# The even layer of a two-block transformer kernel: three stages merged into one that works between the halves of its projection

## What is computed

```
h = x @ w_in                                   # 1024 x 2816
qa, ka, va, ga, qb, kb, vb = split(h)          # qa, ka, va, ga, qb: 512 columns each; kb, vb: 128 each
qa, ka = rope(qa), rope(ka) * 128 ** -0.5      # 4 retention heads of 128
ya = bidirectional_retention(qa, ka, va, decay_logit)
ya = group_norm(ya) * gn_gain * silu(ga)
qb, kb = rope(qb) * 64 ** -0.5, rope(kb)       # 8 query heads of 64, 2 key heads
yb = window_attention_with_sink(qb, kb, vb, sink_logit)
return concatenate([ya, yb]) @ w_out
```

## Time and profile before

| | us |
|---|---|
| median of 3 runs | 2055.55 |
| lowest, highest | 2055.08, 2060.99 |
| the profiled execution | 2063.12 |
| its span, first to last instruction | 2061.2 |
| PE, DVE, ACT, POOL busy in the span | 1800.1, 686.5, 421.5, 81.6 |
| PE's mean granted clock, of full speed | 0.935 |

### The profile page before, as it was taken

One profiled execution on the slowest core, in us unless ns is written; L12 is line 12 of the kernel. 1 busy time (PEld: TensorE's weight loads), 2 busy tenths in 40 slices (PEclk: granted clock), 3 DMA queues, 4 the chain that ended last, 5 costly groups with the idle time before them and its releaser, 6 DMA issues. The chain is left out here.

```text
span 2061.2 us, 20607 instructions
## 1 busy us (share of the span) xinstructions
PE 1800.1 (87%) x8544; PEld 966.4 (47%) x8544; DVE 686.5 (33%) x1313; ACT 421.5 (20%) x673; POOL 81.6 (4%) x60
## 2 busy tenths in 40 slices
PE   7999896995799997945879999988867999999895
PEld 6784454793455554425544444333344443333331
DVE  3656334355333334038322222212124122221223
ACT  2321315441312221013021111111121211111111
POOL 0000001401100000030000000000001000000000
PEclk9999997897899998976779999999987999999998
DMA  5344320007399992520689999999885899999995
GB/s 193 130 176 143 122 82 4 1 1 299 126 386 400 404 405 90 183 106 1 237 369 423 423 423 423 424 423 424 370 355 193 339 423 424 423 423 424 423 423 245
DMA packets 100016, 581.48 MB, mean 282 GB/s; under 512 B 23947, under 2 KB 26251, under 8 KB 34893
## 3 DMA queue, kind: packets, MB, share of 16 engines
q1 hardware_dynamic: 87997, 577.81, 68.6%
q10 hardware_dynamic: 11920, 2.26, 0.6%
HBM read 577.39 MB, written 2.62 MB: 281 GB/s over the span
## 5 line engine op out<-in xcount | busy, mean ns | idle before, releaser
L1717 PE MATMUL up_ps_l<-pool,hT 128*64 128x512 f32 x640 | 143.5, 597 | 13.8 <-DMA pool<-in_expert_w_up 13.8
L1717 PE MATMUL gate_ps_l<-pool,hT 128*64 128x512 f32 x640 | 141.4, 593 | 6.6 <-DMA pool<-in_expert_w_gate 5.3
L446 PE MATMUL proj_ps<-pool,hT 128*128 128x512 f32 x320 | 140.2, 598 | 5.6 <-DVE pool L684 5.6
L1740 PE MATMUL y_ps_l<-pool,hidden_l 128*64 128x512 f32 x640 | 142.6, 596 | 2.2 <-ACT hidden_l L1803 1.4
L1870 DVE SCALAR_TENSOR_TENSOR y_low_l<-y_ps_l,slot_gate_l,y_high_l 128x512 fp32r<-128x512 f32 x64 | 47.0, 751 | 251.3 <-ACT y_high_l L1813 251.3
L438 PE MATMUL proj_ps<-hT,pool 128*128 128x256 f32 x512 | 111.9, 380 | 0.0
L438 PEld LDWEIGHTS proj_ps<-hT,pool 128*128 128x128 f32 x512 | 96.9, 190 | 14.8 <-issue 1.8
L1860 DVE TENSOR_TENSOR hidden_l<-hidden_l,up_ps_l 128x512 f32<-128x512 f32 x32 | 22.0, 688 | 245.0 <-PE up_ps_l L1717 245.0
L446 PEld LDWEIGHTS proj_ps<-pool,hT 128*128 128x128 f32 x320 | 61.4, 192 | 81.3 <-issue 74.6
L1717 PEld LDWEIGHTS gate_ps_l<-pool,hT 128*64 128x64 f32 x640 | 45.5, 137 | 98.5 <-issue 87.2
L1717 PEld LDWEIGHTS up_ps_l<-pool,hT 128*64 128x64 f32 x640 | 43.6, 137 | 99.9 <-issue 77.8
(11 more groups left out here) (502 smaller groups left out, 2707.7 us busy)
## 6 DMA issues: line engine op xcount, KB each, us to landing
pool<-in_expert_w_gate SPq DMA_DIRECT2D x40, 2048.0 KB, 32.4
pool<-in_expert_w_up SPq DMA_DIRECT2D x40, 2048.0 KB, 30.2
pool<-in_expert_w_down SPq DMA_DIRECT2D x40, 2048.0 KB, 32.1
pool<-in_w_in_blocks SPq DMA_DIRECT2D x18, 2048.0 KB, 7.7
pool<-in_moe_w_gate SPq DMA_DIRECT2D x12, 2048.0 KB, 12.4
pool<-in_moe_w_up SPq DMA_DIRECT2D x12, 2048.0 KB, 11.9
pool<-in_moe_w_down SPq DMA_DIRECT2D x12, 2048.0 KB, 11.7
gate_room<-in_expert_w_gate SPq DMA_DIRECT2D x12, 2048.0 KB, 29.8
```

The costliest lines, as they stand in the source:

```text
L446: last = mm(pp[:, n % 2, j * W:(j + 1) * W], k.hT[:, c, j * P:(j + 1) * P], wbuf[n % 2][:, c, :], start=(c == 0), stop=(c == KC - 1))
L1717: last = mm(out[e * CAP:(e + 1) * CAP, 0:H], xg(part * r + c)[:, at:at + CAP], ex.weights(i, e, c), start=(part + c == 0), stop=(part == e ...
L1740: last = mm(Y[e * CAP:(e + 1) * CAP, n], hidT[:, part * r + c, e * CAP:(e + 1) * CAP], ex.weights(i, e, c)[:, n * W:(n + 1) * W], start=(p ...
```

## The change

`stage_even_project`, `stage_even_mix` and `stage_norm_t` become one stage, `stage_even`. Its parts:

- The projection goes by cuts in another order (`EVEN`: qb, kb and vb together as kv, qa, ka, va, ga), and each cut by halves: the product of one token tile is one half, it has one bank, and ScalarE copies it alone (`half_out`). `load_even` therefore loads the columns of qb ahead. A half waits until the half two before it was copied.
- Rotation is done by halves on VectorE and GpSimd when their half has come. Temporaries are smaller (128 x 256), the instructions for qa and ka now cover 256 columns instead of 512 for both together.
- Between halves TensorE does the turning, scores and products of the attention and the retention, in a fixed order (below).
- The masked scores get their maximum per head (L2212); the subtraction of the maximum goes into the exponential's bias, and its sum comes from the exponential's accumulator, 16 exponentials of 256 columns in place of one of 4096.
- The group norm uses the batch norm instructions per head and tile (L2246, L2247) directly from PSUM; centring and gain are one instruction per head and tile (L2252), the last scaling and the product with silu(ga) another (L2265). silu is applied when ga's half is copied.
- Mixed rows are turned at the stage's end and copied by VectorE and ScalarE.
- The output weights are loaded after the fifth weight block was issued, ahead of the sixth. Small vectors and tables are loaded first.

The core of the diff (the rest renames or moves):

```
+EVEN = (("qb", 4 * W, W), ("kv", 5 * W, 2 * WIN_KV * WIN_D), ("qa", 0, W), ("ka", W, W), ("va", 2 * W, W),
+        ("ga", 3 * W, W))
...
-            stage_even_project(k)
-            stage_even_mix(k)
-            stage_norm_t(k, "mix2", k.mix, None)
+            stage_even(k)
...
+                def half(b, j):
+                    n = block_of[b]
+                    width = EVEN[n][2]
+                    if j == 0:
+                        pe.wait_ge(s_w[n % 3], 16 * (n // 3 + 1) + (16 if n % 3 == 0 else 0))
+                    if 2 * n + j >= 2:
+                        pe.wait_ge(s["half_out"], 2 * n + j - 1)
+                    for c in range(KC):
+                        last = mm(PB[(2 * n + j) % 2][:, 0:width], k.hT[:, c, j * P:(j + 1) * P], w[n % 3][:, c, 0:width],
+                                  start=(c == 0), stop=(c == KC - 1))
+                    last.then_inc(s["half_product"], 1)
...
+                half("ka", 1)
+                half("va", 0)
+                rotation_done("ka", 1)
+                pe.wait_ge(s["win_masked"], WIN_H)
...
+                def exps(g):
+                    act.wait_ge(s["win_max"], g + 1)
+                    for h in range(4 * g, 4 * g + 4):
+                        for j in range(NJ):
+                            ins = nc.scalar.activation(sc[:, h, j], sc[:, h, j], ACT.Exp, bias=neg[:, h, j:j + 1],
+                                                       accum_out=total[:, h, j:j + 1])
+                        ins.then_inc(s["win_exp"], 1)
...
+                half_out("qa", 1)
+                exps(0)
+                half_out("ka", 0)
+                exps(1)
+                half_out("ka", 1)
+                half_out("va", 0)
...
+                rotate("qa", 0)
+                rotate("qa", 1)
+                masked(0)
+                rotate("ka", 0)
+                masked(1)
+                rotate("ka", 1)
+                dve.wait_ge(s["win_exp"], WIN_H)
```

More of the change, by code:

```diff
@@ L2107, in stage_even_mix, with load_even @@
-def stage_even_mix(k):
-    nc, i = k.nc, k.i
[L2111 to L2117, removed]
+def load_even(k, sp):
+    sp.dma_start(k.norm_f_row[:], k.i["norm_f_w"].broadcast_to([P, D])).then_inc(k.s_even0, 16)
+    sp.dma_start(k.w_even0[:], k.i["w_in_even"].rearrange("(p c) n -> p c n", c=KC)[:, :, 4 * W:5 * W]).then_inc(
+        k.s_even0, 16)
@@ new lines, in distances @@
+                def distances():
+                    dve.wait_ge(s["lg_ln"], 1)
+                    o(ts(lgt[:], lgt[:], 0.0, None, ALU.min))
+                    o(tt(lgt[:], lgt[:], lga[:], ALU.subtract))
+                    for h in range(RET_H):
+                        d = dm[:, h].rearrange("p a t -> p (a t)")
+                        o(ts(d, ahead, lgt[:, h:h + 1], None, ALU.mult))
+                        stt(out=d, in0=behind, scalar=lgt[:, RET_H + h:RET_H + h + 1], in1=d,
+                            op0=ALU.mult, op1=ALU.add).then_inc(s["dist"], 1)
@@ new lines, in _ @@
+                half_out("kv", 1)
+                half_out("qa", 0)
+                for n in range(3):
+                    act.wait_ge(s["win_turned"], n + 1)
+                    got = M[n][:].rearrange("p (m t) -> p m t", m=2)
+                    if n < 2:
+                        copy(wT[:, 2 * n:2 * n + 2], got, WIN_D ** -0.5).then_inc(s["win_turned_out"], 1)
+                    else:
+                        copy(wT[:, 4:5], got[:, 0:1]).then_inc(s["win_turned_out"], 1)
+                half_out("qa", 1)
@@ L2305, in _ @@
             @block.tensor
             def _(pe):
-                mm = nc.tensor.matmul
-                pe.wait_ge(s["rotated"], 2)
-                turns = turn_list()
-                for n, (b, place, cols) in enumerate(turns):
-                    for j in range(NJ):
-                        last = nc.tensor.transpose(pb[b][:, (place + j) * P:(place + j + 1) * P], cols(j), k.table("ident"))
-                    if n == len(turns) - 1 or turns[n + 1][0] != b:
-                        last.then_inc(s["turned"], 1)
@@ L2315, in _ @@
-                pe.wait_ge(s["turned_out"], 7)
+                mm, turn, ident = nc.tensor.matmul, nc.tensor.transpose, k.table("ident")
+                def half(b, j):
[9 more added lines that the diff above has]
+                    last.then_inc(s["half_product"], 1)
@@ new lines, in _ @@
+                half("qb", 0)
+                half("qb", 1)
+                half("kv", 0)
+                half("kv", 1)
+                half("qa", 0)
+                rotation_done("kv", 1)
+                for n in range(5):
+                    for j in range(NJ):
+                        last = turn(M[n // 2][:, (2 * (n % 2) + j) * P:(2 * (n % 2) + j + 1) * P],
+                                    rot[:, j, 2 * W + n * P:2 * W + (n + 1) * P], ident)
+                    if n % 2 or n == 4:
+                        last.then_inc(s["win_turned"], 1)
@@ new lines, in _ @@
+                half("va", 1)
+                pe.wait_ge(s["ret_turned_out"], 4)
+                pe.wait_ge(s["win_exp"], WIN_H)
+                for h in range(WIN_H):
+                    if h >= 4:
+                        pe.wait_ge(s_po[h % 2], (h - 4) // 2 + 1)
+                    for sj in range(NJ):
+                        for j in range(NJ):
+                            last = turn(M[h % 4][:, sj * T + j * P:sj * T + (j + 1) * P],
+                                        sc[:, h, j, sj * P:(sj + 1) * P], ident)
+                    last.then_inc(s["p_turned"], 1)
```

362 lines of the change are left out of this document (189 added, 173 removed).

## The result

| | before | after |
|---|---|---|
| median, us | 2058.27 (4 runs beside) | 2003.19 (4 runs) |
| lowest, highest | 2055.08, 2063.53 | 2001.47, 2007.42 |
| the profiled execution, its span | 2063.12, 2061.2 | 2002.44, 2000.5 |
| PE busy in the span | 1800.1 | 1785.5 |
| PE's mean granted clock | 0.935 | 0.951 |

The changed kernel takes 0.972 of the time (95% interval 0.9702 to 0.9739), 55 us less. The forecast was 2002.2 in a range of 1994 to 2014, so the time came out 1.0 us above it.

A forecast was written before the change was run, and what follows sets the result against it. TensorE's queue, busy 1800 of 2061 us, was taken to bound the kernel. Work of 111.5 plus waits, clock loss, last copy and gaps gave 119.3 against 172.6; 53.3 off the 2055.55 median gave 2002.2, range 1994 to 2014.

The forecast's parts named there:

- Turns: TensorE's 74 transposes in the stage: 16 at half clock (3.4 us) and 58 at full (7.5), 10.9 against 15.9 before.
- Window product: TensorE's 64 records of 64 columns in the stage: 7.7 us at full clock, against 13.92 at half clock before.
- The wait at the rotation of ka: TensorE idles ahead of L2390 until ka's second half is rotated: 3.6 us, from 888.6 to 892.2.
- rival (c): Chain of maxima and exponentials is longer, 0.59 us an exponential and 0.1 more per link: +4, 2006 us; chance 0.12.
- The clock behind that wait: After the wait ahead of L2390 the clock is at half: 1.3 us lost in sixteen transposes, 1.0 in va's half.
- The end: After ga's last product: 1.2 us of wait and 1.0 for the last transposes' copy; small hand-over gaps add 1.0.
- rival (d): Chain of maxima and exponentials is hidden altogether, by shorter links: -6, 1996 us; chance 0.08.
- Group norm: VectorE's 11.1 us after the retention product hide under TensorE's window product and ga's second half, 14.6, with 3.5 to spare.
- (a): Clock falls in the window product: +5 with half of it hit, +9 in full, 2007 to 2011 us; chance 0.17.
- (b): Transposes let the clock fall in the 32 turns of softmaxed scores: +6, 2008 us; chance 0.06.
- (e): Slower than before: breaks at small groups keep TensorE at half clock through the stage, 38 us more, 2094; chance 0.02.
- (f): Gain is given back behind the stage, if the weight stream has its own date: within 0.3% of before; chance 0.01.

The follow-up runs named there:

- the copy ahead: Changed kernel with ScalarE's copy of ka's second half issued ahead of the exponentials of heads 4 to 7: 1999.17 us, ratio 0.9706 to the kernel before.
- all halves first: Changed kernel with all twelve projection halves done first and attention and retention behind them, rotation still beside the halves: 2019.66 us, ratio 0.9798 to the kernel before.
- the wait ahead of the window product: Changed kernel with one TensorE wait added between retention product and window product, for the group norm's reciprocal: 2016.42 us.
- rotation held back: The kernel with all halves first, with VectorE and GpSimd rotating only once the last half is copied: 2035.51 us, ratio 0.9872 to the kernel before.

## Why the prediction was right, and where its sum was off

The mechanism is the one forecast: nothing ahead of L2375, one wait, ahead of L2390, ended by the rotation; hidden group norm; full clock in the window product; the expert stream moved as a block. The stage was forecast at 119.3 to its last copy and measured 112.55 (822.55 to 935.10). Term by term:

- **Projection, scores, retention product:** 78.9 + 14.0 forecast; 79.3 and 14.3 by the times from one group to the next. Halves cost 0.4 at most, where the forecast had nothing.
- **Turns:** 10.9 forecast; 8.5, of which the ten took 1.1, the sixteen of L2390 1.8 (3.4 forecast), the 32 of L2402 3.5, the last sixteen 2.2. Off because the sixteen kept the full clock, and because the 0.13 was misread from the earlier trace rows: 1.04 for eight is a busy time, with the modelled latency of the last in it. In the changed kernel eight transposes (L1404) also show as 1.05, but the next product starts 0.89 after the first of them (956.08 to 956.97), so 0.11 each, as in the longer rows.
- **Window product:** 7.7 forecast, 7.1 measured. The same misreading: from start to start the 32 records of 128 columns (L2417) take 3.57 and the 64 of 64 columns 7.10, 0.11 each in both.
- **The wait at the rotation of ka:** 3.6 forecast, 1.54 measured. TensorE came 1.0 later than walked (889.6, not 888.6), mostly because the window scores took 3.65 for each 16 records and not 3.2. The rotation was over 1.2 earlier (891.0, not 892.2). In the chain, VectorE began to mask at 864.28 and not at 865.2; its rotation of ka's first half, 256 columns, took 0.42, 0.83 and 0.83 in place of three times 0.92; masks and maxima 0.2 less for four heads; the exponentials 0.49 each and not 0.44. So rival (c) had a true part in it, 16 x 0.05 = 0.8 us, and was outweighed.
- **The clock behind that wait:** this is the step that failed. The prediction said that it falls, for 1.3 in the turns and 1.0 in va's half. It stayed at 1.00 in the three profiles of the changed kernel (above, 853.3 to 935.1). The step took the one row in which the clock fell 2.4 us after the last work and charged a wait of 3.6; at 1.54 there was nothing to charge, so it hangs on the step before it. Whether a wait of 3.6 at this place would have cost it wasn't tried. What the prediction called the cost of the wait, 5.9, was 1.5.
- **The end:** 1.2 of wait, 1.0 of copy and 1.0 of small gaps forecast; 1.02, 0.72 and nothing that the timeline shows.

In sum 2.3 less of work and 4.5 less of waits: 119.3 - 6.8 = 112.5. The stage lost 60.0 us and not 53.3.

**Then why was 2002.2 so near to 2003.19?** By luck: two errors met. The stage's gain was put 6.7 too low, and the time that it was taken off was too low as well. The difference was taken off the median shown, 2055.55, which lay 7.6 below the profiled execution; later sets of runs of the same kernel gave 2058.27, 2062.34 and 2063.38. Taken off the profiled execution's 2063.12, a difference of 53.3 gives 2009.8, against 2002.44 for the profiled execution of the changed kernel; that is still inside the range. The end of rival (d), chain hidden and -6, describes the stage's length better than the forecast does, though its mechanism (no wait) is not what the trace of the changed kernel shows; it is what the copy ahead makes true.

**The cover of the first transposes.** VectorE was forecast to be through with kv at about 848; the rotation of kv ended at 848.14, 5.0 before the ten transposes. The walk had qb's first half at 831.4, which forgot a part of the cold start (its copy begins at 832.75), but that changed nothing behind it.

**Group norm.** Forecast: 3.5 us to spare. VectorE began at 917.37 and ended its first four mixed products at 926.12 + 1.13 = 927.3; ga's second half ended at 931.2. 3.9 to spare.

**Rivals.** (a) and (b) didn't happen in the changed kernel, and the product made twice and the turns made three times refute them with a margin. On (b), the Trainium skill, page "TensorE: Matmul & The Clock Gate", section Part 4: PE-mode transpose, says that transposes don't count as busy for the clock. No run here agrees: 96 of them held it for 10.6 us, and before the change it rose in a stretch that held nothing else. (e), half clock throughout, has only the cold start's 6.2 us to its name. (f): from L1396 to the end it is as long as before, within 1.7. The next stage's first 48 products gain 1.9 (22.78 to 20.84), which the prediction did not name; of this at most 1.7 is seen at the end (1065.5 to between 1063.8 and 1065.1). That the loads, issued at the same distance from the stage's start, take up the rest is argued, not shown.

## What to carry to other kernels

When stages follow each other with chains of small work at their heads, issue that work on the other engines in the columns' own order, piece by piece: here, taken away in this order, 16 of 60 us came from interleaving TensorE's own work, 15 from rotation done under the projection, and 29 from the rest of what was brought forward or shortened, above all that TensorE no longer waits for tables and for the rotation of columns it doesn't need yet. Then look in each engine's queue for a step that others wait for and that stands behind work nobody waits for yet: one exchange took away the last wait. Price a wait with the half clock that it can bring: in these stages every wait of 4.9 us or more brought it, and 4.90 cost 14.4. Take as a group's length the time from its start to the next one's, not its busy time. And take a difference off an execution whose stages were read, not off the median of a few.

## What the runs showed of the hardware

- **A wait's price has a step in it.** 1.54 us cost 1.5 and left the clock at 1.00; 4.90 cost 14.4, with the half clock behind it. Between them, with all halves first, 2.89 us stood ahead of sixteen turns: the clock was still 1.00 through the wait, the first eight took 1.15, close to full clock, and the next eight 1.94, at half. Two stretches of that kernel, the first and the last eight:

```profile
945.30:946.50 1.20, 1.18 (x9) 1.07 (x10) 1.01 (x4) 0.44 (x1) 0.00 (x0) 0.95 0.00 0
946.50:948.40 1.90, 1.85 (x8) 1.45 (x8) 0.70 (x2) 0.76 (x2) 0.00 (x0) 0.50 0.00 0
```

- **How soon the clock falls varies, and no run here shows what sets it.** In the kernel before it fell 2.4 us after the last work. With the wait ahead of the window product it fell some 3.5 us after the last work (estimated from the mean of 0.86 over the 4.90 us), though the retention product was the last work in both. With all halves first it was 0.96 in the last 2 us of work, which had waits of 0.85 and 0.32 ahead of it, and 0.50 from the first moment of the 5.23 us wait.
- **Holding and raising the clock are not the same.** 14.4 us of products of 64 columns at full clock held it, 13.9 us of them at half clock did not raise it (0.50 over 922.2 to 936.0); ga's half behind them did, some 2 us into it (0.50 over 936.0 to 937.0, 1.00 from 938.0). The window scores show the same: they held a full clock for 6.3 us before the change, and with rotation held back 13.17 us of them at half clock did not raise it (0.50 over 912.4 to 925.5).
- **VectorE and GpSimd slow each other down when both rotate.** In the rotation of qb in the changed kernel, VectorE's instructions of 128 columns took 0.28 or 0.29 while GpSimd was idle, mostly 0.50 while it worked (840.29 to 843.41), and 0.29 again behind it. GpSimd's of 128 columns took 0.45 or 0.46 beside them, and up to 0.79 beside VectorE's instructions of 512 columns for the distances. With 256 columns on both, VectorE's first took 0.42 and GpSimd's beside it 0.96, the next two 0.83 and 0.79. The prediction's 0.92 was between its rows, and a little high.
